# A decoder layer on one Trainium2 core: expert blocks of 160 rows with a column-tiled rest in place of blocks of 192

## What is computed

```python
def moe(x, lp):                                   # x: (1104, 1024)
    scores = jax.nn.sigmoid((x @ lp['router_w']).astype(jnp.float32))
    _, idx = lax.top_k(scores + lp['router_bias'].astype(jnp.float32), TOP_K)     # 8 of 64
    gate = jnp.take_along_axis(scores, idx, axis=-1)
    gate = gate / jnp.sum(gate, axis=-1, keepdims=True) * ROUTED_SCALE
    # every token's row goes to its 8 experts; y = swiglu(row; expert) * gate, summed over the 8
    return routed + swiglu(x, lp['w_sh_gate'], lp['w_sh_up'], lp['w_sh_down'])
def swiglu(x, w_gate, w_up, w_down):              # w_gate, w_up: 1024x256, w_down: 256x1024
    return (jax.nn.silu(x @ w_gate) * (x @ w_up)) @ w_down
```

## Time and profile before

| | |
|---|---|
| median of 3 runs | 2700.27 us (2699.69 to 2703.95) |
| the profiled execution | 2703.4 us |
| its span, first to last instruction | 2701.4 us |
| mean granted TensorE clock | 0.95 |
| PE, DVE, ACT, POOL busy | 2435.6, 1306.9, 1050.7, 663.4 us |
| moved by DMA | 394.95 MB, 146 GB/s over the span |
| from 1542.88 to 2647.62 us | the experts' stage |

### The profile page before, as it was taken

The page is one execution under the profiler, slowest core; times in us unless marked ns, Lnnn a source line. Parts: engine busy times, 40 slices in busy tenths (PEclk is TensorE's granted clock), DMA queues, the critical chain, the costliest instruction groups (busy, mean ns, idle before and its releaser), DMA issues. The chain is left out here.

```text
span 2701.4 us, 39475 instructions
## 1 busy us (share of the span) xinstructions
PE 2435.6 (90%) x14550; PEld 1812.3 (67%) x14550; DVE 1306.9 (48%) x2582; ACT 1050.7 (39%) x1706; POOL 663.4 (25%) x574
## 2 busy tenths in 40 slices
PE   7899799899967799999995789999999999999990
PEld 4456566564356466665553378899898998999980
DVE  0544355100176001011662267777777777777764
ACT  1055433100142000000120056666666666666652
POOL 0022321000041000000243024444444444434433
PEclk9989999899978899999997989999999999999995
DMA  3000043200010401001130399999999999999964
GB/s 135 0 12 2 17 175 124 98 32 0 2 35 2 169 31 47 23 23 45 32 113 27 112 291 281 282 288 287 279 283 281 288 284 280 284 286 288 287 163 160
DMA packets 113772, 394.95 MB, mean 146 GB/s; under 512 B 41590, under 2 KB 51142, under 8 KB 85254
## 3 DMA queue, kind: packets, MB, share of 16 engines
q1 hardware_dynamic: 78390, 269.06, 28.4%
q0 software_dynamic: 35296, 124.70, 18.7%
HBM read 325.16 MB, written 69.13 MB: 146 GB/s over the span
## 5 line engine op out<-in xcount | busy, mean ns | idle before, releaser
L2128 PE MATMUL banks<-split 128*128 128x384 f32 x1792 | 538.3, 363 | 0.0
L2242 DVE TENSOR_TENSOR split<-rest,split 128x2048 fp32r<-128x2048 f32 x192 | 438.9, 2286 | 113.3 <-ACT split L2186 113.3
L2126 PE MATMUL banks<-split 128*128 128x192 f32 x2048 | 482.8, 256 | 0.0
L2148 PE MATMUL banks<-split 128*128 128x512 f32 x1536 | 406.6, 407 | 17.5 <-ACT rest L2199 13.6
L2126 PEld LDWEIGHTS banks<-split 128*128 128x128 f32 x2048 | 389.2, 192 | 2.7
L2186 ACT CAST split<-rest 128x2048 fp32r<-128x2048 f32 x192 | 359.2, 1904 | 65.8 <-DMA rest<-in_w_exp_gate 60.8
L1587 PE MATMUL banks<-big 128*128 128x368 f32 x1152 | 358.4, 474 | 14.8 <-DMA big<-in_w_merge 14.8
L2076 POOL DMA_INDIRECT y_rows<-rest x128 | 263.8, 2061 | 340.2 <-ACT rest L2199 299.9
L2128 PEld LDWEIGHTS banks<-split 128*128 128x128 f32 x1792 | 338.9, 189 | 0.0
L2148 PEld LDWEIGHTS banks<-split 128*128 128x128 f32 x1536 | 276.2, 190 | 73.0 <-ACT rest L2199 17.5
L1587 PEld LDWEIGHTS banks<-big 128*128 128x128 f32 x1152 | 219.9, 191 | 153.0 <-issue 16.6
(11 more groups left out here) (338 smaller groups left out, 3036.9 us busy)
## 6 DMA issues: line engine op xcount, KB each, us to landing
rest<-in_w_exp_gate SPq DMA_DIRECT2D x64, 1024.0 KB, 9.0
rest<-in_w_exp_up SPq DMA_DIRECT2D x64, 1024.0 KB, 6.8
rest<-in_w_exp_down SPq DMA_DIRECT2D x64, 1024.0 KB, 7.5
big<-in_w_merge SPq DMA_DIRECT2D x8, 1536.0 KB, 6.7
big<-in_w_cols SPq DMA_DIRECT2D x11, 512.0 KB, 3.3
x_rows<-big SPq DMA_DIRECT2D x9, 512.0 KB, 11.9
y_rows<-big SPq DMA_DIRECT2D x9, 512.0 KB, 2.6
big<-in_x_cols SPq DMA_DIRECT2D x3, 1472.0 KB, 17.2
```

The lines of the kernel that those rows point to most:

```text
L2126: ins = pe.matmul(PS[:, banks[f], 0:CAP], wr[:, s, j, LO, at:at + 128], x[:, k, 0:2], start=False, stop=False)
L2128: ins = pe.matmul(PS[:, banks[f], 0:2 * CAP], wr[:, s, j, HI, at:at + 128], x[:, k], start=False, stop=(k == KD - 1))
L2148: ins = pe.matmul(PS[:, DBANK[c]], hr[:, a, f, HALF * hf:HALF * hf + 128], wr[:, s, DOWN, b, at:at + 512], start=(f == 0 and j == 0), stop ...
L2242: dve.tensor_tensor(wr[:, s, j, LO], raw[:, s, j], wr[:, s, j, HI].bitcast(F32), ALU.subtract).then_inc(parted[j], 1)
```

## The change

Blocks are 160 rows: 128 main rows and 32 of rest. For the main rows the stationary side is now the rows (128 of them), and gate and up weights together are a moving side of 512 columns: 24 fp32r products for gate and up, 12 for down. The 32 rest rows are multiplied in plain fp32 from the raw weights, each product in one of four column tiles of 32 columns (four quarters of gate and up, and four quarters of the output of down, on different partitions). The gate weight is now multiplied into the hidden rows, for which a third copy of the table entries, `wi`, is loaded; hidden rows are transposed by PE (`turn_h`). The loop is skewed: in the turn of block n PE makes gate and up of block n+1, turns the rows of n+2 and makes down of n. Table entries take two DMAs, `wi` three. SP's, POOL's, ACT's and DVE's orders are new. Gathers and scatters have a bounds check at T - 1 so that entries of padding are skipped, and the padding rows of `x1_rows` and `y_rows` go. POOL's small copies of the prompt attention are spread over its units. The diff, cut (old lines of the experts' stage are left out, they are printed above):

```diff
-CAP = 192
-HALF = CAP // 2
+CAP = 160
...
+        def pick(w):
+
+            if w < 8:
+                p, e = w // 2, w % 2
+                c = TAIL + NEW * w
+                own.link(pool.tensor_copy(S.qs_c[:, p, 64 * e:64 * (e + 1)].rearrange("p (h t) -> p h t", h=HEADS), S.qlat[:, :, c:c + NEW]))
+            elif w == 8:
+                own.link(pool.tensor_copy(S.qt_c.rearrange("p (h t) -> p h t", h=HEADS), S.qlat[:, :, 0:TAIL]))
+            elif w < 17:
+                h = w - 9
+                own.link(pool.tensor_copy(S.qt_r[0:ROPE, TAIL * h:TAIL * (h + 1)], S.qh[NOPE:K, h, T - LAST:T - LAST + TAIL]))
+            elif w < 49:
+                h, p = (w - 17) // 4, (w - 17) % 4
+                c = T - LAST + TAIL + 2 * NEW * p
+                dst = S.qs_r[0:ROPE, p].rearrange("p (e h t) -> p e h t", e=2, h=HEADS)[:, :, h]
+                own.link(pool.tensor_copy(dst, S.qh[NOPE:K, h, c:c + 2 * NEW].rearrange("p (e t) -> p e t", e=2)))
+
         for w in range(U):
             pool.wait_ge(rinv_ready, w + 1)
...
                 pool.wait_ge(o_full, (w - 4) // 2 + 1)
             pool.tensor_scalar(diag[:, w % 4], S.ident, sums[:, w:w + 1], None, ALU.mult).then_inc(diag_ready, 1)
-        for p in range(4):
-            for e in range(2):
-                c = TAIL + NEW * (2 * p + e)
-                own.link(pool.tensor_copy(S.qs_c[:, p, 64 * e:64 * (e + 1)].rearrange("p (h t) -> p h t", h=HEADS), S.qlat[:, :, c:c + NEW]))
-        own.link(pool.tensor_copy(S.qt_c.rearrange("p (h t) -> p h t", h=HEADS), S.qlat[:, :, 0:TAIL]))
-        for h in range(HEADS):
-            src = S.qh[NOPE:K, h, T - LAST:T]
-            own.link(pool.tensor_copy(S.qt_r[0:ROPE, TAIL * h:TAIL * (h + 1)], src[:, 0:TAIL]))
-            for p in range(4):
-                dst = S.qs_r[0:ROPE, p].rearrange("p (e h t) -> p e h t", e=2, h=HEADS)[:, :, h]
-                own.link(pool.tensor_copy(dst, src[:, TAIL + 2 * NEW * p:TAIL + 2 * NEW * (p + 1)].rearrange("p (e t) -> p e t", e=2)))
+            pool.wait_ge(diag_ready, w + 1)
+            pick(w)
...
 
     @block.tensor
...
-        sp.dma_start(S.x1_dram[T:T + 128], S.x1[:, 0]).then_inc(x1_out, 16)
-        sp.dma_start(S.x1_dram[T + 128:T + CAP], S.x1[0:CAP - 128, 1]).then_inc(x1_out, 16)
-        sp.wait_ge(x1_out, 16 * (NT + 2))
+        sp.wait_ge(x1_out, 16 * NT)
         sp.wait_ge(shared_in, 16)
...
-        own.did(dve.tensor_copy(S.pairs_i[0:1], cols[0:1, 7:8]))
+        own.did(dve.tensor_copy(S.pairs_i[0:1, 0:1], cols[0:1, 7:8]))
+        own.did(dve.tensor_scalar(S.pairs_i[0:1, 1:2], cols[0:1, 7:8], -1.0, None, ALU.add))
         dve.wait_ge(tab_full, 1)
         own.link(dve.tensor_copy(S.blocks_i[0:1, :, EXPERTS:2 * EXPERTS], PS[0:1, 3, 0:256].rearrange("p (a b) -> p a b", a=2)[:, :, 0:EXPERTS]))
...
-        for j, n in enumerate((4, 4, 3)):
-            sp.wait_ge(y_out[j], 16 * n)
+        for j in range(3):
+            sp.wait_ge(y_out[j], 16 * 3)
 
...
+        def entries(dst, sems, s, first, twice=False):
+            src = S.table[bass.ds(first, CAP)]
+            sp.dma_start(dst[:, s, 0:2].bitcast(I32), src[0:MAIN]).then_inc(sems[s], 16)
+            for j in range(2 if twice else 1):
+                sp.dma_start(dst[REST * j:REST * (j + 1), s, 2:4].bitcast(I32), src[MAIN:CAP]).then_inc(sems[s], 16)
...
+        starts = [first_slot(s) for s in range(2)]
         for s in range(2):
-            entries(gi, gi_in, s, first_slot(s))
+            entries(gi, gi_in, s, starts[s])
+        weights(0, GATE, 0)
+        sp.wait_ge(xg_in[0], 32)
+        weights(0, UP, 0)
         for s in range(2):
+            entries(wi, wi_in, s, starts[s], True)
+        weights(1, GATE, 1)
+        weights(1, UP, 1)
+        weights(0, DOWN, 0)
         with sp.Fori(0, last) as it:
             first = [first_slot(2 * it + s) for s in range(4)]
+            e = [expert(2 * it + 1 + s) for s in range(3)]
             for s in range(2):
                 n = 2 * it + s
+                sp.wait_ge(rest_full, n + 1)
+                weights(s, GATE, e[s + 1])
+                weights(s, UP, e[s + 1])
                 sp.wait_ge(xg_in[s], 32 * (it + 1))
                 entries(gi, gi_in, s, first[2 + s])
-                for j in range(3):
-                    sp.wait_ge(parted[j], n + 1)
-                    weights(s, j, e[s])
                 sp.wait_ge(si_free[s], it + 1)
                 entries(si, si_in, s, first[s])
+                sp.wait_ge(h_made, 2 * n + 2)
+                entries(wi, wi_in, s, first[2 + s], True)
+                sp.wait_ge(part_copied, 3 * n + 2)
+                weights(1 - s, DOWN, e[s])
...
+            for hf, p in enumerate((MAIN, REST)):
+                pool.indirect_dma_start(out=xg[0:p, s, hf], out_offset=None, in_=S.x1_dram,
+                                        in_offset=bass.IndirectOffsetOnAxis(ap=gi[0:p, s, 2 * hf:2 * hf + 1].bitcast(I32), axis=0),
+                                        bounds_check=T - 1, oob_is_err=False).then_inc(xg_in[s], 16)
+
+        def scatter(s, turn, first=False):
+            if s or not first:
+                pool.wait_ge(y_out[1 - s], 32 * (turn + s))
+            pool.sem_inc(si_free[1 - s], 1)
+            pool.wait_ge(part_copied, 3 * (2 * turn + s) + 6)
             pool.sem_inc(passed, 1)
+            for hf, p in enumerate((MAIN, REST)):
+                pool.indirect_dma_start(out=S.y_dram, in_=y[0:p, s, hf], in_offset=None, compute_op=ALU.add,
+                                        out_offset=bass.IndirectOffsetOnAxis(ap=si[0:p, s, 2 * hf:2 * hf + 1].bitcast(I32), axis=0),
+                                        bounds_check=T - 1, oob_is_err=False).then_inc(y_out[s], 16)
+
+        def body(it, more, first=False):
             for s in range(2):
-                if not ends:
-                    pool.wait_ge(xr_full, 4 * (2 * it + s + 1))
-                    gather(s, it + 1)
-                scatter(s, it)
-            pool.wait_ge(y_out[1], 32 * (it + 1))
-            pool.sem_inc(si_free[1], 1)
+                if s < more:
+                    pool.wait_ge(xr_full, 2 * (2 * it + s + 2))
+                    gather(*ahead(s, it, 3))
+                scatter(s, it, first)
...
+        pool.wait_ge(xr_full, 2)
+        gather(0, 1)
+        body(0, 2, first=True)
+        with pool.Fori(1, before_last) as it:
+            body(it, 2)
+        body(before_last, 1)
+        body(last, 0)
+        pool.wait_ge(y_out[1], 32 * (last + 1))
...
+            if not first:
+                pe.wait_ge(xr_parted[r], n)
+            if before is not None:
+                pe.wait_ge(part_copied, 3 * before + 2)
+            for j in range(4):
+                k = 4 * r + j
+                ins = pe.transpose(PS[:, XBANK[r], 128 * j:128 * (j + 1)], xg[:, s, 0, 128 * k:128 * (k + 1)], S.ident)
             ins.then_inc(xr_full, 1)
...
+        def turn_rest(s, turn_):
+            for k in range(KD):
+                ins = pe.transpose(PS[:, EBANK, 256 + REST * k:256 + REST * (k + 1)], xg[0:REST, s, 1, 128 * k:128 * (k + 1)],
+                                   S.ident[0:REST, 0:REST])
+            ins.then_inc(xrest_full, 1)
+
+            pe.wait_ge(xrest_copied, n + 1)
+            for j in (GATE, UP):
                 pe.wait_ge(parted[j], n + 1)
+            for k in range(KD):
+                for w in (GATE, UP):
+                    for f in range(2):
+                        q, at = REST * (2 * w + f), DEXP * k + 128 * f
+                        ins = pe.matmul(PS[q:q + REST, RBANK, 0:128], x_rest[:, k], raw[:, s, w, at:at + 128],
+                                        start=(k == 0), stop=(k == KD - 1), skip_group_check=True)
+            ins.then_inc(rest_full, 1)
+            for r in range(2):
+                pe.wait_ge(xr_parted[r], n + 1)
+            for k in range(KD):
+                for j, (a, b) in enumerate(PRODUCTS):
+                    ins = pe.matmul(PS[:, MBANK].rearrange("p (j n) -> p j n", j=2), xr[:, a, k],
+                                    wr[:, s, GATE:UP + 1, b, DEXP * k:DEXP * (k + 1)],
+                                    start=(k == 0 and j == 0), stop=(k == KD - 1 and j == 2))
+            ins.then_inc(main_full, 1)
...
+        def turn_h(s, turn_):
+            pe.wait_ge(h_made, 2 * (2 * turn_ + s) + 2)
+            for f in range(2):
+                pe.transpose(PS[:, HBANK, MAIN * f:MAIN * (f + 1)], h[:, 128 * f:128 * (f + 1)], S.ident)
+            pe.transpose(PS[:, HBANK, 2 * MAIN:2 * MAIN + 2 * REST], h_rest[0:2 * REST], S.ident[0:2 * REST, 0:2 * REST]).then_inc(hT_full, 1)
+
...
+            if c == 0:
                 pe.wait_ge(parted[DOWN], n + 1)
+                pe.wait_ge(hr_parted, n + 1)
+            pe.wait_ge(part_copied, 3 * n + 2 * c + 1)
+            for f in range(2):
+                at = DM * f + 512 * c
+                for j, (a, b) in enumerate(PRODUCTS):
```

(123 more changed lines are left out.)

243 lines of the change are left out of this document (68 added, 175 removed).

## The result

The changed kernel takes 2916.45 us (median of four runs, 2908.09 to 2921.47) against 2702.11 for the kernel before beside it (2699.69 to 2711.47): ratio 1.078, interval 1.075 to 1.082. It is 214 us slower; the forecast was 111 slower, and 2916 lies outside its range. The profiled execution has a span of 2914.9 us. First its page: busy line, slices, then groups with busy us and mean ns, and the idle time before them.

What follows compares the result with a forecast made beforehand. The prediction took a ring through SP and POOL, 17.2 us a step, as the bound: 31 + 69 x 17.2 + 6 = 1224 us against 1104.7, +119; with attention -8, +111 in total: 2811 us, range 2650 to 2875.

Steps and rivals of the forecast that it cites:

- PE's 14.0 us: Experts' stage: PE's work per block after the change, with tile-shape changes and the loop's turn, 14.0 us.
- I take four at once: 1.7 and 0.85 us: Rest rows on PE: four fp32 column tiles overlap, 1.7 us for gate and up, 0.85 for down.
- Rival 3: PE: fp32 column tiles don't overlap (21.7 us, 3121 us in all), or pauses let its clock fall; chance 0.06.
- The ring: SP and POOL: every step waits for table entries landing behind whole weights in SP's queue; 17.2 us a step.
- Rival 1: Experts' stage: PE stays the bound, as tables overtake weights or the ring has slack; 14.0 us, 2590; chance 0.14.
- rival 2: SP's wait for si_free: the ring holds but the scatter fits beside the weights; 14.9 to 15.4 us, 2652; chance 0.14.
- 14.65 plus the scatter: One turn of SP's step: issues, landing of gi, gathers, table loads, DOWN and hand-overs, 14.65 us before the scatter's share.
- DOWN and four hand-overs 0.65: End of SP's turn: issuing DOWN and four hand-overs takes 0.65 us.
- I take 2.5: The scatter's share of the turn, what it takes of the DMA engines during the landing: 2.5 us, bounds 0 and 3.7.
- The two gathers, 2.2: POOL's two gather issues in the turn: 0.94 + 0.30 + 0.93 = 2.2 us.
- Second ring: DOWN's landing, cast, subtraction, hidden rows, DVE's copy, `down_rest`, then DOWN again: 14.9 us, binding less than the first.
- The sign turned at a step of 15.6: Experts' stage: the change turns from gain to loss at a step of 15.6 us (31 + 69 x 15.6 + 6 - 8 = 1105).

Runs made afterwards that it cites:

- e12: e10 with every scatter cut to 2 + 2 rows; 2591.18 us, ratio 0.953 to the kernel before.
- e3: The changed kernel with the table entries for the next gather issued ahead of GATE and UP; 2691.62 us, ratio 0.992 to the kernel before.
- e8: The changed kernel with every scatter cut to 2 + 2 rows; 2770.58 us, ratio 1.020 to the kernel before.
- e2: The changed kernel with SP's seven register loads at the loop's top done twice, the second set unused; 3046.6 us, ratio 1.123.
- e1: The changed kernel with SP's loop turned by half a step, so its register loads stand behind a table issue; 2886.18 us, ratio 1.064.
- e6: e3 with DVE's copy of the next block's rest rows moved ahead of DOWN's subtraction and the hidden product; 2682.54 us, ratio 0.988.
- e4: The kernel before with only the attention stage's 49 small POOL copies spread one to a diagonal; 2703.31 us, ratio 0.997.
- e11: The changed kernel with its padding moved again, all 160 rows gathered and scattered; 2968.25 us, ratio 1.094 to the kernel before.
- e7: e6 with SP's register loads moved behind the entries' issue, as in e1; 2668.51 us, ratio 0.983 to the kernel before.
- e10: e7 with DOWN's cast behind the main sigmoid, and its subtraction behind the hidden product and the copy; 2659.53 us, ratio 0.979.

## Why the forecast was wrong in size

- **Blocks, PE's work.** 70 blocks: right. PE's 14.0 us: 13.57 in e12, where nothing else stops it; the 24 products take 5.73 to 5.78 us against 24 x 0.239 = 5.74. "I take four at once: 1.7 and 0.85 us" was the author's estimate, a quarter of 6.8 and 3.4, and no row of before shows it with 128 or 256 moving columns. Measured were 1.95 us for the 32 products of gate and up, 64 records, in the changed kernel, and 1.07 for the 8 of down, 16 records, in e12. So the four column tiles do overlap here: both times are far below the 6.8 and 3.4 of one after the other. The 1.0 for seven changes of tile shape and the 0.26 for the loop's turn were estimates too, and no run here prices either alone. The kernel before shows one such change: from 357.97 on, the loads for 16 records come in pairs, 0.43 us from pair to pair, and the next shape starts 3.59 us after the first, 0.15 more than eight pairs need. Without the 1.0 the sum was 13.0, with it 14.0: the measured 13.57 stands between them.

```profile
2033.19 1.95 PE L2168 MATMUL banks<-rest 128*32 128x128 f32 x64
2035.08 5.78 PE L2175 MATMUL banks<-split 128*128 128x512 f32 x24
```
```profile
2016.80 1.07 PE L2222 MATMUL banks<-rest 128*32 128x256 f32 x16
```

- **Rival 3's other half, the clock.** The granted clock did fall, from 0.95 to 0.91, and PE paid for it. Behind PE's wait for the copy six products of down take 2.93 us where six before it took 1.63, and the granted clock from 2028 to 2033 is 0.66:

```profile
2024.69 1.63 PE L2196 MATMUL banks<-split 128*128 128x512 f32 x6
2028.63 1.21 PE L2209 MATMUL banks<-rest 128*32 128x256 f32 x16 [2.31 <-DVE rest L2332]
2029.77 2.93 PE L2196 MATMUL banks<-split 128*128 128x512 f32 x6
```

  PE is busy 15.0 us a block in the changed kernel (161.44 of 200 at 18.62 a turn) against 13.57 in e12. In this kernel it costs next to nothing: SP waits for PE 0.6 us in 1000, from 1700 to 2700.

- **The ring.** The mechanism is shown by e3: take the entries out from behind the weights and 233 us go. Rival 1 falls for this kernel, and so does rival 2 (the scatter does not fit beside the weights, e8).
- **The step that failed: the sum of the turn, 14.65 plus the scatter, in its term "DOWN and four hand-overs 0.65".** 3.38 us were measured for this piece (0.62 in one step, 6.25 in the next). The term left out SP's register loads at the loop's top, which issue nothing and stand in no row of busy time; e2 shows 3.8 us of the pause for seven of them. Before the change SP waited 540.8 us of 900 for DVE, so they could hide there (no run takes them out of that kernel); the change put SP on the path, and everything that SP does came onto it. The other pieces of the turn together are 1.3 less than forecast: 1.6 less at the gathers and 0.3 less at the landing, 0.6 more at the table issues.
- **The pause and the landing are not separate losses.** Taken out alone the pauses are worth 39 us (e1), not 69 x 2.73 = 188, as the landing rises from 10.3 to 11.8. Even so e1's turn of 18.1 is 0.9 above the forecast's: without the pause the forecast would have been too low by its landing, 10.6. That the measured mean landing, 10.3, agrees with 10.6 is in part luck: it is 8.4 behind a pause that the forecast did not have and 12.1 behind none.
- **"I take 2.5" for the scatter**: 2.3 in the mean, 3.3 in a standing queue (e8). With the 0.7 more of the weights' own landing this gives the 12.1 where no pause goes ahead.
- **The two gathers, 2.2**: 0.63, as SP is let go while POOL still issues them. This error has the other sign and hid 1.6 us of the rest.
- **Second ring, 14.9, binds less**: e3's period of 14.81 seems to meet it, but e6 broke its link and won 11 us only. The number matched by accident; other waits, for DOWN's landing, for the table and for the hidden product, stood at the same place.
- **PE idle 2 to 4 us before `down_rest`**: 202.6 us over 70, 2.9. **DMA share 0.75**: 0.74. **Landing 9 to 12**: 10.3 in the mean. **Attention -8**: -7 in e4 (3 to 11). **Padding 0.6 a block**: 0.59 by e11's 41 us.

The sign turned at a step of 15.6; e3, e6, e7 and e10, at 14.6 to 15.0, lie on the other side, and e8, at 16.3, on the slower side, as that figure says.

## What to carry to other kernels

When a change makes an issuing engine wait for the landing of what it issued itself, write down the whole turn of that ring, and count what the engine does that is no instruction of work: register loads, the loop's turn. Try small control data ahead of bulk data in the same queue; here that order alone was worth 8% of the kernel (e3). In an engine's written order put last what is needed last (DOWN's cast; e10's 11 us are not clear of the noise), but check first that what moves ahead is not itself late.

## What was not expected of the hardware

No group of the profile's busy time shows them; in SP's timeline they are a gap between two issues, 5.85 us from DOWN to GATE at 2035.27 in the changed kernel against 0.60 at 2054.48.
- In the changed kernel the landing of the entries was 12.1 us in the steps without a pause and 8.4 in those behind a pause (6.2 in the mean over the loop). In e2 it was 7.1 behind the pauses of 10.1, but 13.4 in the other steps, and the mean stayed: 10.2 against 10.3.
- With the scatters of 128 + 32 rows (126 of them real in the mean) cut to 2 + 2, the small load on SP's queue landed 3.3 us sooner where no pause goes ahead (12.1 to 8.8) and 1.3 sooner behind a pause (8.4 to 7.1) (e8).
- In the changed kernel PE waited 2.31 us until 2028.63. From 2028 to 2033 its granted clock was 0.66, and six products took 2.93 us, against 1.63 for six before the wait; from 2033 to 2043 the clock was 1.00.
